# A ring of three weight tiles in the first stage of a hybrid encoder layer, split two tiles ahead

## The reference

```python
h = rms_norm(x, g_mix[l])                    # over the 1024 channels of a token
proj = h @ w_in[l]
q = proj[..., RWKV_COLS:RWKV_COLS + ATTN_WIDTH]                      # 512 columns, 8 heads of 64
k = proj[..., RWKV_COLS + ATTN_WIDTH:RWKV_COLS + ATTN_WIDTH + KV_COLS]   # 128 columns
v = proj[..., RWKV_COLS + ATTN_WIDTH + KV_COLS:]                     # 128 columns
q = rms_norm(q.reshape(B, T, ATTN_Q_HEADS, HEAD_DIM), q_gain)
k = rms_norm(k.reshape(B, T, ATTN_KV_HEADS, HEAD_DIM), k_gain)
```

## Time and profile before

| what | value |
|---|---|
| median of 3 executions | 3061.29 us (3059.34 to 3065.22) |
| profiled execution, first to last instruction | 3048.9 us |
| median less the profiled span | 12.4 us |
| first stage in the profiled execution | 0 to 215.8 us |
| PE busy over the whole span | 2789.9 us (92%) |
| DVE, ACT and POOL busy over the span | 2058.0, 1363.4 and 665.4 us |

### The profile page before, as it was taken

One profiled execution on the slowest core, in us unless ns is written; L12 is line 12 of the kernel. 1 busy time (PEld: TensorE's weight loads), 2 busy tenths in 40 slices (PEclk: granted clock), 3 DMA queues, 4 the chain that ended last, 5 costly groups with the idle time before them and its releaser, 6 DMA issues. The chain is left out here.

```text
span 3048.9 us, 62296 instructions
## 1 busy us (share of the span) xinstructions
PE 2789.9 (92%) x24610; PEld 2226.5 (73%) x24610; DVE 2058.0 (68%) x3096; ACT 1363.4 (45%) x2618; POOL 665.4 (22%) x843
## 2 busy tenths in 40 slices
PE   7889989998659999996999789999799999799999
PEld 4655578884459999994667678888588888588887
DVE  6867623235586666634446878888888888587786
ACT  4547711116635555543244434455444454344443
POOL 5447700000037787721232000000000000000000
PEclk9999999999869999998999899999899999899999
DMA  4432222324794444334654132222122221726401
GB/s 131 149 94 50 49 80 68 77 55 162 286 285 148 139 144 143 95 110 160 193 176 152 68 116 77 83 83 80 56 83 80 83 77 66 278 98 225 158 28 56
DMA packets 302490, 361.25 MB, mean 118 GB/s; under 512 B 119977, under 2 KB 202409, under 8 KB 302082
## 3 DMA queue, kind: packets, MB, share of 16 engines
q1 hardware_dynamic: 297314, 352.01, 35.6%
q10 hardware_dynamic: 4896, 5.38, 0.5%
HBM read 254.16 MB, written 103.14 MB: 117 GB/s over the span
## 5 line engine op out<-in xcount | busy, mean ns | idle before, releaser
L99 PE MATMUL up_p<-up_b_hi,up_a_hi 128*128 128x512 f32 x1232 | 490.3, 398 | 43.2 <-ACT inv L2295 23.3
L100 PE MATMUL up_p<-up_b_lo,up_a_hi 128*128 128x512 f32 x1232 | 490.1, 398 | 0.0
L101 PE MATMUL up_p<-up_b_hi,up_a_lo 128*128 128x512 f32 x1232 | 489.6, 397 | 0.0
L99 PEld LDWEIGHTS up_p<-up_b_hi,up_a_hi 128*128 128x128 f32 x1232 | 233.7, 190 | 103.7 <-ACT inv L2295 24.6
L100 PEld LDWEIGHTS up_p<-up_b_lo,up_a_hi 128*128 128x128 f32 x1232 | 233.6, 190 | 56.0
L101 PEld LDWEIGHTS up_p<-up_b_hi,up_a_lo 128*128 128x128 f32 x1232 | 233.5, 189 | 55.4
L2738 ACT CAST down_a_hi<-down_a 128x512 fp32r<-128x512 f32 x154 | 96.0, 623 | 259.5 <-PE down_p_x L101 143.4
L2250 ACT CAST up_a_hi<-up_a_sum 128x512 fp32r<-128x512 f32 x132 | 81.4, 617 | 224.3 <-DVE up_a_sum L2409 147.3
L2753 DVE TENSOR_TENSOR down_a_lo<-down_a,down_a_hi 128x512 fp32r<-128x512 f32 x154 | 106.3, 690 | 97.5 <-ACT down_a_hi L2738 97.5
L2320 ACT ACTIVATE up_con<-up_raw,vecs_sb 128x1023 f32<-128x1023 f32 (+1 forms) x88 | 109.7, 1246 | 127.4 <-DVE up_raw L2479 83.9
L2485 DVE SCALAR_TENSOR_TENSOR up_con<-up_raw,vecs_sb,up_con 128x1023 f32<-128x1023 f32 (+1 forms) x88 | 113.1, 1285 | 65.9 <-ACT up_con L2320 65.9
(11 more groups left out here) (298 smaller groups left out, 7356.9 us busy)
## 6 DMA issues: line engine op xcount, KB each, us to landing
up_a_raw<-in_w_up SPq DMA_DIRECT2D x172, 256.0 KB, 2.7
rec_inp<-gate_chunks SPq DMA_DIRECT2D x64, 512.0 KB, 3.7
down_a<-in_w_down SPq DMA_DIRECT2D x88, 256.0 KB, 8.7
down_b<-act_out SPq DMA_DIRECT2D x88, 256.0 KB, 9.0
first_w<-in_w_attn SPq DMA_DIRECT2D x24, 512.0 KB, 3.5
rkv_chunks<-rwkv_project_mix SPq DMA_DIRECT2D x12, 1024.0 KB, 6.5
gate_chunks<-gates_out SPq DMA_DIRECT2D x3, 4096.0 KB, 12.2
act_out<-up_con SPq DMA_DIRECT2D x22, 512.5 KB, 2.6
```

What stands on the lines that cost most here:

```text
L99: pe.matmul(out, w_hi, x_hi, start=start, stop=False, skip_group_check=True)
L100: pe.matmul(out, w_hi, x_lo, start=False, stop=False, skip_group_check=True)
L101: return pe.matmul(out, w_lo, x_hi, start=False, stop=stop, skip_group_check=True)
```

## The change

The weight tiles lie in a ring of three places (WR = 3). The raw tile `w` and its low part `w_lo` share one place: `first_w` is allocated and given back, and `w_lo` is allocated over it, so POOL writes the low part over the raw weights it reads. The three rings take as much memory as the three pairs before. Item g+2 is split at the head of item g, on ACT and on POOL; item 1 is split ahead of the loop. A load must wait until the projection that read the old low part is done (`projected`), where it waited before until the low part two items back had been made (`w_lo`). The engines, the operations, their shapes and their number stay as they are.

```diff
+    WR = 3
-        w = sb("w", [P, 2, KD, P])
-        w_hi = sb("w_hi", [P, 2, KD, P], F32R)
-        w_lo = sb("w_lo", [P, 2, KD, P], F32R)
+        w_hi = sb("w_hi", [P, WR, KD, P], F32R)
+        with nc.sbuf_tensor("first_w", [P, WR, KD, P], F32) as w:
+            pass
+        w_lo = sb("w_lo", [P, WR, KD, P], F32R)
...
                 def load_w(g):
-                    done(sp, "w_lo", g - 1)
-                    sp.dma_start(w[:, g % 2], K.d["w_attn"][g % MT]).then_inc(S[f"w_in{g % 2}"], 16)
+                    done(sp, "projected", g - WR + 1)
+                    sp.dma_start(w[:, g % WR], K.d["w_attn"][g % MT]).then_inc(S[f"w_in{g % WR}"], 16)
...
                 def split(g):                                  (ACT)
-                    done(act, f"w_in{g % 2}", 16 * (g // 2 + 1))
-                    done(act, "projected", g - 1)
-                    nc.scalar.copy(w_hi[:, g % 2], w[:, g % 2]).then_inc(S["w_hi"], 1)
+                    done(act, f"w_in{g % WR}", 16 * (g // WR + 1))
+                    done(act, "projected", g - WR + 1)
+                    nc.scalar.copy(w_hi[:, g % WR], w[:, g % WR]).then_inc(S["w_hi"], 1)
...
                 high(0, range(KD))
+                split(1)
                 def body(g, n, m):
-                    if g + 1 < ITEMS:
-                        split(g + 1)
+                    if g + 2 < ITEMS:
+                        split(g + 2)
```

More of the change, by code:

```diff
@@ L141, in first_block @@
             + ["x_squared", "x_added", "x_summed", "x_rooted", "x_inverted", "scaled", "high", "low",
-               "w_in0", "w_in1", "w_hi", "w_lo", "projected", "copied", "squared", "summed", "rooted", "inverted", "normed",
+               "w_in0", "w_in1", "w_in2", "w_hi", "w_lo", "projected", "copied", "squared", "summed", "rooted", "inverted", "normed",
                "turned", "v_copied"])
@@ L265, in body @@
                             done(pe, "low", n * KD + k + 1)
-                        mm = product(pe, p_proj[:, g % 2], w_hi[:, g % 2, k], w_lo[:, g % 2, k],
+                        mm = product(pe, p_proj[:, g % 2], w_hi[:, g % WR, k], w_lo[:, g % WR, k],
                                      K.h_hi[:, k, toks(n)], K.h_lo[:, k, toks(n)], k == 0, k == KD - 1)
@@ L376, in split @@
                     done(pool, "w_hi", g + 1)
-                    tt(w_lo[:, g % 2], w[:, g % 2], w_hi[:, g % 2].bitcast(F32), ALU.subtract).then_inc(
+                    tt(w_lo[:, g % WR], w[:, g % WR], w_hi[:, g % WR].bitcast(F32), ALU.subtract).then_inc(
                         S["w_lo"], 1)
```

## The result

| | before | changed |
|---|---|---|
| median | 3064.9 us (20 executions) | 3070.83 us (20 executions) |
| ratio to before | | 1.0023, 95% interval 1.0015 to 1.0031 |
| the same, measured a second time | | 1.0023, 1.0013 to 1.0032 |
| first stage ends in the profile at | 215.8 us | 220.0 us, and 222.1 in the second profile |

The ratio stands for 7 us (4.6 to 9.5). The range forecast was 3055.5 to 3066.5, and the likeliest case was no change. The rival whose mechanism came true had 9%: the raw tile late for ACT, 3069.5 us. That this number lies so near to 3070.83 is in part luck. It adds 8.2 us to the median of three executions, 3061.3, while twenty gave 3064.9; the stage itself grew by 4.2 us in one profile and by 6.3 in the other.

A forecast was written before the change was run, and what follows sets the result against it. The prediction took a DVE, ACT, DVE ring to set the first stage's 47 us per tile. Its terms, +2.1 + 2 x (0.2 - 0.4 + 0.1) - 2.6 = -0.7 us, gave 3060.6 us, range 3055.5 to 3066.5.

The forecast's parts named there:

- A ring DVE, ACT, DVE: First stage: DVE and ACT waiting on each other set the 47 us per token tile, not PE's weight waits.
- The squares of the middle tiles, +0.2: Two middle tiles: item 9's split ahead of the squares on ACT delays them +0.2 us per tile, bounds 0 and +1.8.
- The third rival: First stage: raw tile late for ACT in every tile if landing exceeds 5.5 us; +8.2, 3069.5 us, chance 9%.
- First tile, +2.1: First tile: ACT's split(3) waits for its load ahead of the squares, costing +2.1 us, bounds +1.0 and +5.2.
- The four `low`: Middle tiles, DVE: the first four low start sooner but meet POOL's three scale; -0.4 us per tile, bounds -2.4 and +0.6.
- The second four: Middle tiles, DVE: the second four low already meet scale and change within 0.1; taken at +0.1 us per tile.
- The last tile, -2.6: Last token tile: shorter normed of item 20 and slightly earlier head_root(20) end the stage 2.6 us sooner, bounds -0.3 and -4.0.
- The clock: Rival, attention start behind the stage: a lengthened or removed half-clock stretch would cost or return 4.4 us; chance 4%.
- The 12.4 us around the span: Whole kernel: time added to the profiled span, taken against the 3061.3 us median, to reach the forecast time.
- the forecast of -0.7: First stage: sum of all terms, -0.7 us, giving 3060.6 us for the kernel; chance 71%.
- The second rival: Middle tiles: DVE's idle before low gained whole, DVE and POOL not in each other's way; 3055.8 us, chance 11%.

The follow-up runs named there:

- The loads left out: Changed kernel without the loads of weight tiles 3, 9 and 15, part of h_hi split instead: ratio 0.9996 to the kernel before, stage end 215.2 us.
- the filler run: Changed kernel plus 8 unused matmuls at each of two places where PE idles: ratio 1.0019 to the kernel before, stage end 219.3 us.
- the ring split one ahead: Changed kernel with its ring of three, but the split again one tile ahead: ratio 0.9992 to the kernel before, stage end 215.0 us.
- the run without filler: Changed kernel, squares ahead of the split in item m = 1, last tile's ACT splits behind take: ratio 0.9997 to the kernel before, stage end 216.3 us.

## Why the prediction was wrong, point by point

**What bounds the stage: right.** A ring DVE, ACT, DVE, with PE's stalls beside it. All of PE's later waits for w_lo went away and the turn got longer.

**The squares of the middle tiles, +0.2: this step failed.** The forecast let the load of tile 9 go at 81.9 and land after 3.5 to 5.5 us, with ACT free at 85.67, and took nearly the early end of that: a wait of 0.2 us. Measured, ACT's cast waited 2.10 us for tile 9 and 1.80 for tile 15, and DVE's idle grew by 2.2 and 1.9 us, above the bound of +1.8. The loads left out put it to the test: 3.19 us of idle again.

The issue time is not what was wrong. It was 84.52 and not 81.9, but 1.9 of these 2.6 us are the delay from the first tile, which moved `take` as well (84.70 to 86.64). Only the rest, from projection 6 running at the lower clock, brought the load nearer to `take`: projection 6 ended 1.98 us behind the last h_lo, where it had ended 1.08 behind it before. What was wrong is the landing. It was taken as a time that runs from the issue, whatever stands ahead. The table of the filler run shows it tied to the burst of eight x loads, 6.2 to 7.2 us behind the last of them, while ACT is free some 4.9 us behind it (87.73 against 82.86). An issue at the forecast's 81.9, 1 us behind the burst of before, would have met a landing after 5.2 to 6.2 us by these rows, which is an estimate. That the burst itself causes the delay was not tested by a run without it.

**The third rival** had this mechanism, but made it hang on a landing above 5.5 us. In the changed kernel the two loads took 5.3 and 4.0 us, and 4.6 and 4.3 in its second profile, and the tile was late each time. Over 5.5 us it was for tile 9 where the load went out right behind the burst: 6.3 us with filler, 6.5 with the ring split one ahead.

**First tile, +2.1: right, with two errors that cancel.** The first sum came 2.5 us later, 3.1 in the second profile. The load went at 36.85, not at 37.5, and landed after 4.1 us, not 3.2 to 3.5.

**The four `low`: right in mechanism.** They took 4.87 us instead of 3.80, and from the first sum to their end it was 30.71 us instead of 30.97: -0.26 for the -0.4 forecast. By the rule of the Trainium skill (SBUF — State Buffer, Who interferes with whom), with full blocking, it would have been +0.6. The trace sides with the partial overlap. The second four, taken at +0.1, came to -0.1.

**The last tile, -2.6: wrong.** Against T2 the end came 1.5 and 0.7 us sooner in the two profiles (79.4 and 80.2 us, against 80.95). The `normed` of item 20 took 0.75 us in place of 2.92, as forecast. But load 23 went out 56.7 us behind T2, against 57.3 before: 0.6 us sooner and not 2.2. Its cast waited 3.57 us, and `head_root(20)` came 1.2 us later behind T2, not 0.3 sooner. Projection 18, with its matmuls at the lower clock, ended at 182.7, 42.1 us behind T2 against 40.9 before. With the cast behind `take` or the load earlier nothing was won, so the cast alone was not the limit.

**The clock: not in the sum.** The forecast had it only behind the stage. Spread over 13 stalls of up to 1.6 us, PE's idle time left the clock at 1.00 in the earlier trace rows. Gathered into gaps of 3 us it did not, and behind each of the four gaps of 2.9 to 3.3 us from 76 to 180 us the clock went to 0.50. The length of a gap alone does not tell: behind the same gap of 1.6 us near 39 us the clock fell in the changed kernel's first profile (0.83 from 36 to 46 us) and stayed at 1.00 in its second. The Trainium skill (TensorE: Matmul & The Clock Gate, What's actually happening) says that the throttled state is the default and that activity releases it; the trace agrees, with 0.50 behind 2.89 us of idle and 1.00 with filler in the gap.

**The 12.4 us around the span: misread.** The execution of 3072.42 us has a span of 3070.6, so 1.8 us lie around it. With these 1.8 us the profiled execution of before would have taken 3050.7 us, less than the shortest of the twenty timed (3059.16); why it was so short is not known. The base of the forecast, the median of three, was 3.6 us below that of twenty. Taken from the right base the forecast of -0.7 would be 3064.2, still 6.6 us below the measured median.

**The second rival's sum: a slip.** Its "less 0.2" stands against the forecast's own small terms, 2 x 0.2 and 2 x 0.1, which would add 0.6: 3056.6 and not 3055.8. No reading hangs on it.

## What to carry to other kernels

To prefetch one step further, ask what stands behind the new wait in the in-order queue of each engine, not only whether the data would be there in time for their use. A load behind a burst in the same queue is not early because it is issued early: read in the trace when loads at that place land, counted from the burst, and not how long a load takes by the median. A buffer shared by raw and derived data makes the load wait for the last reader of the derived data. And short stalls that are taken away on TensorE can come back as a longer one elsewhere, if another ring sets the pace.

## What the hardware showed beside that

- The same load of 512 KB landed in 3.2 us alone (the one at 90.4 us in the changed kernel), in 4.0 to 6.5 us behind eight loads of x (the table of the filler run), and there the longer the sooner it was issued behind them, and in 5.4 us behind two of the bias.
- Idle matmuls, whose result nobody reads, made a stage shorter: 216.3 to 211.4 us, of which 1.9 us lie behind T1, clear of the dip at the start of the run without filler.
- With the same instructions the recurrence took 552.3, 562.0 and 563.9 us in three profiles, more than the whole effect studied. A difference of two single spans says little about a change in one stage; the stage's own end does.
